# 64 more bytes in a small tensor, so that the tensors behind it lie 64 bytes further on

## The chip, the cores and the metric

One core of a Trainium2 chip runs the whole program. The metric is the device time of one execution in microseconds (us); lower is better. Three executions of the kernel before gave 1581.59, 1583.28 and 1583.49 us, a median of 1583.28 us.

## The reference

A chain of two transformer blocks on 256 tokens of width 1024, in float32.

```python
h = h + gla_mixer(rms_norm(h, a_norm), ...)            # gated linear attention, 4 heads
h = h + sqrelu_mlp(rms_norm(h, mlp_norm[0]), w1, w2)   # square(relu(x @ w1)) @ w2, hidden 4096
k_sh, v_sh = shared_kv(h, kv_norm, w_kv, k_norm)
h = h + diff_mixer(rms_norm(h, b_norm), k_sh, v_sh, ...)   # difference of two softmaxes, 8 heads
h = h + sqrelu_mlp(rms_norm(h, mlp_norm[1]), w1, w2)
# second block: three branches that are gated, summed and projected
merged = g0 * conv_branch(...) + g1 * ssd_branch(...) + g2 * windowed_attention(...)
h = h + merged @ w_mix_out
h = h + memory_cross_attention(rms_norm(h), rms_norm(mem), ...)
h = h + sqrelu_mlp(rms_norm(h, norm_mlp), w_mlp_up, w_mlp_down)
```

Nearly all of the arithmetic is in the products with weight matrices: 420 pieces ("chunks") of 1024 x 128 weights.

## The kernel before

**Layout.** Activations are held transposed: 128 partitions, and per partition 8 slices (`KC`) of 256 tokens (`T`). A weight chunk is 8 squares of 128 x 128.

**A product in three parts.** Both operands are split into a high part and a remainder. For each of the 8 slices PE does high weights times high activations (L396) and high weights times low activations (L397), both float32 with 256 columns. Then it does 8 bf16 products of the low weights (L406). A chunk is 16 float32 and 8 bf16 products, each with its own weight load. L440, L441 and L446 are the same three in the second half of an MLP; L423, L424 and L426 are the same three with the roles swapped (activations loaded as weights, weights moving), which is used where the result is wanted with tokens on the partitions.

**The stream of chunks.** SP loads weights into `raw`, a ring of four slabs of two chunks (L356, L368). ACT rounds a chunk to `w_hi` (L942), DVE subtracts to get `w_lo` (L1484), PE multiplies, DVE takes the sum out of PSUM. ACT may run 3 chunks ahead, and a slot of `w_hi` comes free when PE is done with the chunk four back. The order of the work on each engine is written out by hand; each engine's function (from L346 on for SP, then PE, ACT, DVE, POOL) walks through the same stages, with semaphores between them.

**Operand sets.** The activations for the products stand in two sets, XA and XB. Each has `both` (8 slices, each with 256 high and 256 low float32 numbers, so 2048 bytes a slice) and `bf` (8 slices of 512 bytes). ACT writes the high part and `bf` (L948, L949, L951, L952), DVE the low part (L1497, L1499).

**The arena.** All that lives for one stage only is cut out of one tensor, `arena`, of 81920 bytes a partition: masks, queries, keys, values, hidden activations (squared by POOL, L2120), the padded input of the 31-tap convolution, and so on. The convolution reads `c_in[:, i, k:k + T]` for each tap k: rows of 286 numbers (1144 bytes), starting 4 bytes further on with each tap. Six channel slices are done as products on ACT (L1190) and sums on POOL (L2150), two on DVE (L1764). The bias rows of the windowed attention are stored from the arena to DRAM once (L1098, issued from ACT's queue), and POOL fetches them back 16 times with a skew (L2162). The masks (L362) and the memory input are loaded into the arena once.

**Where the tensors lie.** Tensors are placed in the order in which they are declared (L117 to L166), one after the other. By the built program's list, in bytes within a partition:

| tensor | starts at | modulo 1024 | modulo 128 |
|---|---|---|---|
| raw | 16512 | 128 | 0 |
| w_hi | 49280 | 128 | 0 |
| w_lo | 65664 | 128 | 0 |
| H (the residual stream) | 73856 | 128 | 0 |
| con (constants) | 89184 | 96 | 96 |
| hn_sqb | 100096 | 768 | 0 |
| gains (64 bytes) | 104192 | 768 | 0 |
| arena | 104256 | 832 | 64 |
| xa_both | 186176 | 832 | 64 |
| xa_bf | 202560 | 832 | 64 |
| xb_both | 206656 | 832 | 64 |
| xb_bf | 223040 | 832 | 64 |
| small_hi, small_lo | 227136, 228160 | 832 | 64 |

`gains` holds four columns of scaled gains; only `gains[:, 0:4]` is ever written or read.

Of the kernel before, what the change touches and what calls it, by code (L numbers as in the profile page):

```python
# [22 lines left out]
P = 128  # L23
# [89 lines left out]
def program(nc, w_d, par_d, con_d, gm_d, x_d, mem_d, band_d, out_d):  # L113
    ctx = ExitStack()
    with ctx:
        def sb(name, shape, dt=F32):
            return ctx.enter_context(nc.sbuf_tensor(name, shape, dt))  # L117
# [22 lines left out]
        rtok_mem = sb("rtok_mem", [P, NT])  # L140
        hn_sqb = sb("hn_sqb", [P, 2, T])
        hn_rb = sb("hn_rb", [P, 2, T])
        gains = sb("gains", [P, 16])
        ARENA = 20480
        arena = sb("arena", [P, ARENA])
        ps = ctx.enter_context(nc.psum_tensor("ps", [P, 8, 512], F32))
# [2170 lines left out]
```

## Time and profile before

| | |
|---|---|
| median of 3 executions | 1583.28 us |
| the profiled execution | 1579.73 us |
| its span, first to last instruction | 1577.9 us |
| PE busy | 1426.4 us (90%) |
| PE weight loads busy | 1294.0 us (82%) |
| DVE busy | 1035.2 us (66%) |
| ACT busy | 889.3 us (56%) |
| POOL busy | 329.9 us (21%) |
| granted TensorE clock, mean | 0.959 |

The page gives the share of busy time, a row of 40 slices, the chain of work that ended last, and groups of instructions. A duration of an instruction is not its cost where instructions overlap: PE's matmuls are pipelined, and there the distance from one start to the next is what counts. It is read from the timeline.

### The profile page before, as it was taken

How to read it: one execution, taken by the hardware profiler on the slowest of the kernel's cores; microseconds unless marked ns; L12 is line 12 of the kernel's file. 1: busy time of each engine (PE TensorE's matmuls, PEld its weight loads, DVE VectorE, ACT ScalarE, POOL GpSimd, SP SyncE). 2: the span in 40 equal slices, each digit the busy share in tenths (PEclk: the TensorE clock that was granted, in tenths of full speed). 3: DMA queues.
4: the chain of work that ended last, by engine and by line, in shares of the span. 5: the costliest groups of instructions: out<-in, count | busy, mean ns of one | idle time of the engine just before them, and what ended most of it. 6: DMA issues, size and time to landing. Idle time of an engine off the chain costs nothing. (4 is left out here: it accounts for less than half of the span.)

```text
span 1577.9 us, 30012 instructions
## 1 busy us (share of the span) xinstructions
PE 1426.4 (90%) x11488; PEld 1294.0 (82%) x11488; DVE 1035.2 (66%) x1661; ACT 889.3 (56%) x1693; POOL 329.9 (21%) x334
## 2 busy tenths in 40 slices
PE   7987999989879999989877779898898979799999
PEld 6876999988757999989877667777777779599998
DVE  6794755566656666647999755568576666375555
ACT  4434655456556555548988655454565466365553
POOL 2000411132004111126878100004000004051111
PEclk9998999999987999979999989999999989999999
DMA  7320555545713555534434322234434335055552
GB/s 305 132 107 29 189 200 197 186 161 132 216 54 107 194 203 191 187 107 171 151 136 157 128 86 102 86 107 161 137 126 149 124 134 188 27 188 194 204 189 81
DMA packets 35603, 233.72 MB, mean 148 GB/s; under 512 B 4000, under 2 KB 7072, under 8 KB 8352
## 3 DMA queue, kind: packets, MB, share of 16 engines
q1 hardware_dynamic: 31104, 223.75, 39.8%
q10 hardware_dynamic: 3216, 4.19, 1.7%
q0 software_dynamic: 1168, 4.20, 0.9%
q8 instruction: 78, 1.28, 0.3%
q14 instruction: 37, 0.30, 0.1%
HBM read 227.93 MB, written 4.19 MB: 147 GB/s over the span
## 5 line engine op out<-in xcount | busy, mean ns | idle before, releaser
L1484 DVE TENSOR_TENSOR w_lo<-raw,w_hi 128x1024 bf16<-128x1024 f32 x420 | 536.1, 1277 | 242.4 <-ACT w_hi L942 239.0
L942 ACT CAST w_hi<-raw 128x1024 fp32r<-128x1024 f32 x420 | 438.7, 1047 | 351.7 <-PE ps L406 179.3
L396 PE MATMUL ps<-xa_both,w_hi 128*128 128x256 f32 x1808 | 464.9, 297 | 32.6 <-ACT w_hi L942 11.1
L397 PE MATMUL ps<-xa_both,w_hi 128*128 128x256 f32 x1808 | 439.7, 283 | 0.0
L396 PEld LDWEIGHTS ps<-xa_both,w_hi 128*128 128x128 f32 x1808 | 350.9, 194 | 44.1 <-issue 25.0
L397 PEld LDWEIGHTS ps<-xa_both,w_hi 128*128 128x128 f32 x1808 | 351.8, 195 | 0.6
L406 PE MATMUL ps<-xa_bf,w_lo 128*128 128x256 bf16 x1808 | 240.2, 277 | 21.4 <-DVE w_lo L1484 21.4
L406 PEld LDWEIGHTS ps<-xa_bf,w_lo 128*128 128x128 bf16 x1808 | 160.7, 99 | 49.3 <-DVE w_lo L1484 24.8
L440 PE MATMUL ps<-xb_both,w_hi 128*128 128x256 f32 x768 | 188.4, 288 | 0.0
L441 PE MATMUL ps<-xb_both,w_hi 128*128 128x256 f32 x768 | 180.0, 277 | 0.0
L396 PE MATMUL ps<-xb_both,w_hi 128*128 128x256 f32 x576 | 149.7, 299 | 13.5 <-DVE xb_both L1497 7.8
L2120 POOL TENSOR_TENSOR arena<-arena 128x256 f32<-128x256 f32 x96 | 68.2, 710 | 388.6 <-DVE arena L1553 388.6
L440 PEld LDWEIGHTS ps<-xb_both,w_hi 128*128 128x128 f32 x768 | 144.5, 188 | 1.1
L441 PEld LDWEIGHTS ps<-xb_both,w_hi 128*128 128x128 f32 x768 | 144.6, 188 | 0.0
L397 PE MATMUL ps<-xb_both,w_hi 128*128 128x256 f32 x576 | 141.3, 285 | 0.0
L2150 POOL TENSOR_TENSOR arena<-arena 128x512 f32<-128x512 f32 x90 | 127.4, 1417 | 51.1 <-ACT arena L1190 40.3
L396 PEld LDWEIGHTS ps<-xb_both,w_hi 128*128 128x128 f32 x576 | 112.8, 196 | 20.4 <-issue 12.4
L397 PEld LDWEIGHTS ps<-xb_both,w_hi 128*128 128x128 f32 x576 | 112.9, 196 | 0.2
L446 PE MATMUL ps<-xb_bf,w_lo 128*128 128x256 bf16 x768 | 100.5, 274 | 0.0
L2080 POOL TENSOR_TENSOR sumsq<-H 128x256 f32<-128x256 f32 x6 | 3.7, 612 | 400.7 <-DVE H L1521 370.0
L1190 ACT ACTIVATE arena<-arena,par 128x256 f32<-128x256 f32 x180 | 77.6, 497 | 6.6 <-POOL arena L2150 6.6
L406 PE MATMUL ps<-xb_bf,w_lo 128*128 128x256 bf16 x576 | 78.7, 282 | 0.0
(288 smaller groups left out, 1932.9 us busy)
## 6 DMA issues: line engine op xcount, KB each, us to landing
raw<-weights SPq DMA_DIRECT2D x210, 1024.0 KB, 4.8
band<-arena ACTq DMA_DIRECT2D x1, 3072.0 KB, 35.4
arena<-band POOLq DMA_DIRECT2D x8, 256.0 KB, 3.2
arena<-gla_masks SPq DMA_DIRECT2D x1, 1088.0 KB, 15.6
H<-x_t SPq DMA_DIRECT2D x2, 512.0 KB, 4.8
arena<-mem_t POOLq DMA_DIRECT2D x1, 1024.0 KB, 5.2
arena<-band POOLq DMA_DIRECT2D x8, 128.0 KB, 2.6
out_t<-H ACTq DMA_DIRECT2D x8, 128.0 KB, 2.0
```

The costliest lines, as they stand in the source:

```text
L396: mm(ps[:, bank, 0:T], w_hi[:, s, k], X.hi[:, k], start=k == 0, stop=False)
L397: mm(ps[:, bank, 0:T], w_hi[:, s, k], X.lo[:, k], start=False, stop=False)
L406: last = mm(ps[:, bank, 0:T], w_lo[:, s, k], X.bf[:, k], start=False, stop=k == KC - 1)
L440: mm(down_sums(n), w_hi[:, s, i], XB.hi[:, k], start=opens, stop=False)
L441: mm(down_sums(n), w_hi[:, s, i], XB.lo[:, k], start=False, stop=False)
L446: done = mm(down_sums(n), w_lo[:, s, i], XB.bf[:, k], start=False, stop=last and (k, n) == DOWN[j][-1] and j >= 4)
L942: nc.scalar.copy(w_hi[:, j % HI_SLOTS].rearrange("p k n -> p (k n)"), raw[:, j // 2 % RING, j % 2]).then_inc(hi_done, 1)
L1190: A(c_prod[:, a % PRODUCTS, i % 2], c_in[:, i, k:k + T], ACT.Copy, scale=w).then_inc(ca["prod"], 1)
L1484: TT(w_lo[:, j % HI_SLOTS].rearrange("p k n -> p (k n)"), raw[:, j // 2 % RING, j % 2], w_hi[:, j % HI_SLOTS].rearrange("p k n -> p (k n)" ...
L2080: G.tensor_tensor(sumsq[:], src[:, k], src[:, k], ALU.mult).then_inc(sq_step, 1)
L2120: G.tensor_tensor(m_sq[:, j % 2], m_relu[:, j % 2], m_relu[:, j % 2], ALU.mult).then_inc(sq_done, 1)
L2150: G.tensor_tensor(both, both, c_prod[:, a % PRODUCTS], ALU.add).then_inc(ca["add"], 1)
```

## The change

One number: `gains` becomes 32 columns wide instead of 16.

```diff
         hn_sqb = sb("hn_sqb", [P, 2, T])
         hn_rb = sb("hn_rb", [P, 2, T])
-        gains = sb("gains", [P, 16])
+        gains = sb("gains", [P, 32])
         ARENA = 20480
         arena = sb("arena", [P, ARENA])
```

`gains` stays at 104192 and takes 128 bytes. Everything declared after it (arena, XA, XB, small_hi, small_lo) starts 64 bytes later: at 896 instead of 832 modulo 1024, which is 0 instead of 64 modulo 128. `ps`, the accumulator, is another memory and does not move. No instruction is added, removed, reordered or reshaped on any engine: the five engines' lists of instructions are the same row for row.

## Rows read from the trace of the kernel before

**Rows 1.** The page, head and sections 1 and 2.
```profile
span 1577.9 us, 30012 instructions
...
PE 1426.4 (90%) x11488; PEld 1294.0 (82%) x11488; DVE 1035.2 (66%) x1661; ACT 889.3 (56%) x1693; POOL 329.9 (21%) x334
...
PEclk9998999999987999979999989999999989999999
```
**Rows 2.** The page, section 4: the chain that ended last.
```profile
PE 26%; DVE 3%; ACT 2%; issue 1%; DVEq 0%; ACTq 0%
```
**Rows 3.** Windows: busy us (and instructions) of each engine, clock, DMA share, GB/s.
```profile
150.00:350.00 200.00, 195.49 (x1712) 186.81 (x1711) 124.16 (x159) 108.15 (x162) 44.32 (x55) 0.99 0.54 190
350.00:400.00 50.00, 48.24 (x356) 42.75 (x355) 33.47 (x56) 33.69 (x67) 15.40 (x16) 0.94 0.52 115
400.00:480.00 80.00, 65.56 (x441) 49.98 (x439) 48.66 (x122) 45.39 (x140) 0.00 (x0) 0.87 0.41 127
```
**Rows 4.** Timeline, PE in an MLP: start us, us, engine, line, what.
```profile
300.71 1.05 PE L446 MATMUL ps<-xb_bf,w_lo 128*128 128x256 bf16 x8
...
302.07 0.28 PE L396 MATMUL ps<-xa_both,w_hi 128*128 128x256 f32 x1
302.18 0.28 PE L397 MATMUL ps<-xa_both,w_hi 128*128 128x256 f32 x1
...
303.32 0.28 PE L397 MATMUL ps<-xa_both,w_hi 128*128 128x256 f32 x1
...
303.44 1.05 PE L406 MATMUL ps<-xa_bf,w_lo 128*128 128x256 bf16 x8
```
**Rows 5.** One line each: min/median/max ns, first and last start, shapes. Weight loads.
```profile
L396 PEld LDWEIGHTS ps<-xa_both,w_hi x1808: 186/188/337, 10.8 to 1551.1; 128*128 128x128 f32 x181
...
L423 PEld LDWEIGHTS ps<-w_hi,xa_both x144: 186/188/199, 42.9 to 1114.0; 128*128 128x128 f32 x144
```
**Rows 6.** Timeline, PE with the roles swapped: weights move, activations are loaded.
```profile
405.00 0.28 PE L423 MATMUL ps<-w_hi,xa_both 128*128 128x256 f32 x1
...
406.47 0.28 PE L424 MATMUL ps<-w_hi,xa_both 128*128 128x256 f32 x1
```
**Rows 7.** Timeline, PE in the keys of the shared attention.
```profile
361.64 0.28 PE L396 MATMUL ps<-xa_both,w_hi 128*128 128x256 f32 x1
...
363.17 0.28 PE L397 MATMUL ps<-xa_both,w_hi 128*128 128x256 f32 x1
```
**Rows 8.** One line each: the convolution's taps, on ACT and on DVE.
```profile
L1190 ACT ACTIVATE arena<-arena,par x180: 492/495/512, 721.8 to 869.3; 128x256 f32<-128x256 f32 x180
...
L1764 DVE SCALAR_TENSOR_TENSOR ps<-arena,par,ps x58: 470/483/484, 758.4 to 859.8; 128x256 f32<-128x256 f32 x58
```
**Rows 9.** One line each: DVE sums into H, and products into the arena.
```profile
L1521 DVE TENSOR_TENSOR H<-ps,H x32: 415/424/425, 151.0 to 1399.4; 128x256 f32<-128x256 f32 x32
...
L1503 DVE TENSOR_TENSOR arena<-ps,rstd x102: 409/418/426, 32.8 to 1345.6; 128x256 f32<-128x256 f32 x102
```
**Rows 10.** One line each: POOL's squares, from H, and from the arena.
```profile
L2084 POOL TENSOR_TENSOR sqtmp<-H x42: 612/784/789, 154.6 to 1399.9; 128x256 f32<-128x256 f32 x42
...
L2120 POOL TENSOR_TENSOR arena<-arena x96: 612/722/779, 175.4 to 1553.1; 128x256 f32<-128x256 f32 x96
```
**Rows 11.** DMA issues: size of one, median us from issue to landing.
```profile
band<-arena ACTq DMA_DIRECT2D x1, 3072.0 KB, 35.4
...
arena<-gla_masks SPq DMA_DIRECT2D x1, 1088.0 KB, 15.6
```
**Rows 12.** One line each: issue of the bias rows, and the next user of them.
```profile
L1098 ACTq DMA_DIRECT2D band<-arena x1: 357/357/357, 383.8 to 383.8; - x1
...
L2140 POOL MEMSET arena<- x1: 303/303/303, 694.4 to 694.4; 128x240 f32 x1
```
**Rows 13.** Timeline, POOL fetches bias rows: start us, us, and idle before.
```profile
1132.96 0.72 POOL L2162 DMA_DIRECT2D arena<-band  x1 [27.94 <-DVE arena L1990]
1136.66 0.72 POOL L2162 DMA_DIRECT2D arena<-band  x1 [2.98 <-DVE arena L1990]
1147.05 0.72 POOL L2162 DMA_DIRECT2D arena<-band  x1 [9.66 <-DVE arena L1990]
```
**Rows 14.** Timeline, PE after the first MLP: the pauses, and the products behind them.
```profile
349.73 0.55 PE L396 MATMUL ps<-xa_both,w_hi 128*128 128x256 f32 x1 [4.45 <-DVE H L1537]
...
351.82 0.58 PE L396 MATMUL ps<-xa_both,w_hi 128*128 128x256 f32 x1
352.20 0.42 PE L397 MATMUL ps<-xa_both,w_hi 128*128 128x256 f32 x1
```

## Prediction

> **What bounds the kernel now.** I start at the page's head and its busy times: PE works 1426.4 of 1577.9 us, DVE 66%, ACT 56%, POOL 21% [rows 1]. The chain that ended last says the same for the part of the span that it is followed through, some 32%: 26 of these are PE's, 3 DVE's and 2 ACT's [rows 2]. The windows show two kinds of stage. In the first MLP PE is busy 195.49 of 200 us; in the differential attention only 65.56 of 80 us, with a granted clock of 0.87 [rows 3]. The reader should take from this that a change in the matmuls' pace counts in full in the MLPs and in part elsewhere, and that a change in DVE, ACT or POOL counts only in the attention stages and the convolution.
>
> Then the timeline inside an MLP. The group of 8 bf16 products starts at 300.71 and the next one at 303.44, so a chunk takes 2.73 us. From the product at 302.07 to the one at 303.32 are 11 steps: 1.25 / 11 = 113.6 ns from one float32 product to the next [rows 4]. That pace, 16 times per chunk and 420 chunks (6720 float32 products), is what the change could touch at the greatest price: 1 ns on each is 6.7 us if all lay on the path, 3.1 us for the 192 chunks of the three MLPs alone (192 x 16 = 3072 products).
>
> **The change part by part.** It adds and removes no instruction, DMA or wait. What it moves is the start of every operand that lies behind `gains`, from 64 to 0 modulo 128 bytes (from 832 to 896 modulo 1024). So the question is whether any engine's time depends on the start of an operand. The kernel itself contains operands of both kinds, and that is how each term can be read off the trace.
>
> *Moving operand of PE.* Before, XA and XB move (832 modulo 1024) against weights at 128. With the roles swapped, the weights at 128 move, and XA at 832 is loaded. From 405.00 to 406.47 are 13 steps of 1.47 / 13 = 113.1 ns [rows 6], against 113.6 [rows 4]. So a moving operand at 0 modulo 128 runs at the pace of one at 64. I take 0 ns. The bounds: the pace isn't 113.6 everywhere. In the keys' stage 13 steps take 1.53 us, 117.7 ns each [rows 7], with the same two tensors at the same addresses. That can't be a matter of address; what it is the rows don't tell, but it is the nearest price for a slower pace: 4.1 ns. The nearest for a faster one is the bf16 group, whose 8 products take 1.05 us, the last one's 0.27 or 0.28 included: (1.05 - 0.27) / 7 = 111 ns [rows 4], 2.6 ns less. Ends: -2.6 x 3072 = -8 us in the MLPs and -17 us in all; +4.1 x 3072 = +13 us and +28 us.
>
> *Weight loads.* With w_hi as weights the load takes 186/188 ns (least and median), with XA as weights 186/188 ns [rows 5]. Two kinds of start, one duration: 0.
>
> *ACT and DVE.* The taps of the convolution are the best natural experiment here. The 180 products on ACT start at 30 offsets, 4 bytes apart, in six rows that are themselves 1144 bytes apart: every multiple of 4 modulo 128 occurs. They take 492 to 512 ns, with a median of 495; the 58 on DVE take 470 to 484 [rows 8]. The whole spread over all starts is 20 and 14 ns, and a move of 64 bytes only permutes the starts among themselves. DVE's products into the arena (64 modulo 128) take 418 ns, its sums into H (0 modulo 128) 424 [rows 9]. I take 0. As an upper bound I let each of some 400 DVE instructions of this size become 6 ns slower or faster: 2.4 us, nearly all of it beside PE's work.
>
> *POOL.* Squares read from H and from the arena have the same least duration, 612 ns [rows 10]; the medians 784 and 722 are of different stages with different neighbours. I take 0; besides, POOL is idle 79% of the span [rows 1].
>
> *DMAs.* The weights' ring `raw` stands ahead of `gains` and doesn't move, nor do H's input and output. What moves are the masks, the memory input, 16 fetches of bias rows and one store of bias rows. The store takes 35.4 us, the masks 15.6 [rows 11]. The store is issued at 383.8; POOL's next step that waits for it is at 694.4 [rows 12], so it has 275 us to spare, and nothing would be late if it took twice as long. The bias fetches are issued 3.7 and 10.4 us apart, each after a step of DVE two units back [rows 13], and each waits for DVE rather than the other way round. I take 0 on the path. A rule speaks for a small loss here: the Trainium skill, page "DMA: Bandwidth & Descriptors", section "How a descriptor splits into AXI transactions", says that a read that doesn't start at a multiple of 256 bytes begins at the multiple below and pays for the bytes between, in beats of 32. The stored rows are 1536 bytes and start at 160 modulo 256, after the change at 224: 53 beats become 55, and my estimate from that page for the whole store is 35.4 x 2/53 = 1.3 us more. By it the sum would be +1.3 us if the store were on the path, and 0 where it stands.
>
> The sum: 0. For the profiled execution that means 1577.9 + 1.8 = 1579.7 us again. The median of the three runs lies 3.55 us above it; the forecast goes by the median: **1583.3 us**.
>
> **The rivals.** *The matmul's pace gets worse (slower).* After the change moving operands, loaded weights, `raw` and H all start at 0 modulo 128, where before the two that PE reads at the same time differed by 64. If PE reads both sides at once and two reads of one phase disturb each other, the place is the pair L396/L397 and L440/L441, and the price is up to the pace of the keys' stage: +13 us if only the MLPs feel it, +28 us if all do, 1596 to 1611 us, and 1603 as its middle. It decides from 0.5 ns a product on (0.5 x 6720 = 3.4 us). Against it: the weight slices are 512 bytes long, so successive ones start at 128 and 640 modulo 1024, and the pace within a chunk is steady. For it: no row here has both sides at 0 modulo 128 in this kind of product.
>
> *The matmul's pace gets better (faster).* The same place with the other sign: an operand at 64 modulo 128 needs one more access for its last piece, and the float32 pace of 113.6 comes down towards the 111 of bf16. That gives -8 to -17 us, 1566 to 1575 us. Against it: the swapped products move an operand that has the better start already and are no faster [rows 4, 6].
>
> *The clock falls otherwise (either sign).* After the first MLP PE pauses for 4.45 us, and two products behind the pause are 0.38 us apart, more than three times their usual distance [rows 14]; the mean granted clock of the stage is 0.94, against 0.99 in the MLP, and 0.87 in the attention behind it [rows 3]. Some stages hang on such pauses. A few nanoseconds elsewhere may shift where the clock falls: one chunk at three times the distance costs 16 x 0.26 = 4 us. That is an outcome of single executions; it would move the median only if it moved each run the same way: 1579 to 1588 us.
>
> *The change doesn't do what it says.* If other padding took up the 64 bytes, the addresses would be the old ones and the time 1583.3 us, the same as the forecast. The list of the built program's tensors speaks against it, and it costs the forecast nothing.
>
> **How the numbers follow.** About 0.2% (3.2 us) is what a measurement of this kernel can tell from no change; the three runs span 1.9 us. No effect: 0.76. Worse pace 0.09, better pace 0.09. The clock beyond 3.2 us: 0.03 on either side. So faster 0.12, same 0.76, slower 0.12. The forecast is 1583.3 us. The range 1578 to 1589 holds the case of no effect, most of the clock's, and a pace that is off by less than 1 ns; the rest of the two pace cases, some 0.15, stays outside.
>
> **What would show it.** Right: 113.6 ns between float32 products and 2.73 us per chunk in the MLPs, loads at 188 ns, L1190 at 495, L1521 at 424 and L1503 at 418, POOL's least at 612, all as before; PE busy within 3 us of 1426. Wrong: a chunk in an MLP of 2.67 or 2.80 us; or, if the time changes without that, an ACT, DVE or POOL group that reads the arena with a median off by over 5 ns, and its stage longer by as much. If only the stages around the pauses differ, it is the clock.

## The result: 1603.65 us, and the profile after

The kernel with the wider `gains` takes 1603.65 us (median of 4 executions, 1600.13 to 1605.35) against 1583.38 us (4 executions, 1581.59 to 1587.40) of the kernel before: a ratio of 1.0127 [1.0100, 1.0154]. It is 20 us slower, and outside the range of 1578 to 1589.

The page of the execution that was profiled (1605.35 us), head, busy times, clock, chain and two DMA issues:

```profile
span 1603.5 us, 30012 instructions
...
PE 1456.7 (91%) x11488; PEld 1320.0 (82%) x11488; DVE 1034.9 (65%) x1661; ACT 890.0 (55%) x1693; POOL 329.4 (21%) x334
...
PEclk9996999998987999989999989999999989899999
...
PE 25%; DVE 4%; ACT 2%; issue 1%; DVEq 0%; ACTq 0%
...
band<-arena ACTq DMA_DIRECT2D x1, 3072.0 KB, 35.5
...
arena<-gla_masks SPq DMA_DIRECT2D x1, 1088.0 KB, 15.0
```

Against [rows 1], the instructions are the same in number, and DVE, ACT and POOL work as long as before, to within 0.7 us. Only PE works longer: 30.3 us more in its products and 26 us more in its weight loads. The two DMAs take what they took [rows 11]. The mean granted clock of this execution is 0.952 against 0.959, so some of the difference between the two profiled executions is the clock's. But the execution of the changed kernel whose clock was 0.959 too took 1600.13 us, which is 20.4 more than the 1579.73 of the profiled one before.

The timeline of PE in an MLP of the changed kernel (start us, duration us, engine, line, what), to be held against [rows 4]:

```profile
300.86 0.28 PE L440 MATMUL ps<-xb_both,w_hi 128*128 128x256 f32 x1
...
301.93 0.28 PE L441 MATMUL ps<-xb_both,w_hi 128*128 128x256 f32 x1
```

These are 9 steps in 1.07 us, 118.9 ns from one float32 product to the next, where [rows 4] had 113.6. Taken as the mean over the last nine steps of the 16 float32 products of every chunk in the second halves of the MLPs (the "steady pace" from here on), it is 119.4 ns after and 113.3 ns before, and all 96 of these chunks are within 1 ns of it.

The same is seen more cheaply in a group's median duration. One line each, min/median/max ns, of the kernel before:

```profile
L441 PE MATMUL ps<-xb_both,w_hi x768: 276/276/283, 192.9 to 1573.1; 128*128 128x256 f32 x192
...
L424 PE MATMUL ps<-w_hi,xa_both x144: 276/279/284, 43.1 to 1114.2; 128*128 128x256 f32 x144
```

and of the changed kernel:

```profile
L441 PE MATMUL ps<-xb_both,w_hi x768: 278/282/284, 199.7 to 1598.7; 128*128 128x256 f32 x192
...
L424 PE MATMUL ps<-w_hi,xa_both x144: 278/283/284, 43.2 to 1132.1; 128*128 128x256 f32 x144
...
L441 PEld LDWEIGHTS ps<-xb_both,w_hi x768: 187/192/193, 199.6 to 1598.6; 128*128 128x128 f32 x192
L446 PE MATMUL ps<-xb_bf,w_lo x768: 272/273/284, 201.5 to 1599.6; 128*128 128x256 bf16 x192
```

A duration of 276 ns goes with a pace of 113.3, 279 with about 118, 282 or 283 with about 120; it moves by the same few nanoseconds as the pace, though it is more than twice as long. The float32 products are slower in every kind of chunk, and the weight load at L441 takes 192 ns (median) against 188. The bf16 products stay at 273 ns. And the row of L424 before holds a warning that I did not see: its median was 279 and not 276, so the swapped products were slower than the others in the kernel before already.

There is a second warning in that trace. Of the chunks that run at the full clock, not all of one kind have one pace: among 275 whole chunks at L396/L397, 238 run at 113.3 ns and 37 at 117.8, and the keys' stage [rows 7] is among the 37; among 25 swapped ones, 22 run at 117.8 and 3 at 113.3. The two operands lie in the same places modulo 256 bytes in both groups each time. So the addresses alone don't settle the pace of every single chunk. In the second halves of the MLPs, where the chunks follow each other without a pause, all 96 are at 113.3, which is why the steady pace is taken there.

The groups of the other engines whose operands moved:

```profile
L1190 ACT ACTIVATE arena<-arena,par x180: 492/495/513, 738.2 to 885.9; 128x256 f32<-128x256 f32 x180
...
L1503 DVE TENSOR_TENSOR arena<-ps,rstd x102: 410/420/426, 32.8 to 1363.5; 128x256 f32<-128x256 f32 x102
...
L1521 DVE TENSOR_TENSOR H<-ps,H x32: 419/425/425, 156.3 to 1420.5; 128x256 f32<-128x256 f32 x32
...
L2120 POOL TENSOR_TENSOR arena<-arena x96: 612/725/782, 181.7 to 1578.2; 128x256 f32<-128x256 f32 x96
```

None of their medians is off by more than 3 ns from [rows 8, 9, 10].

**The sum.** In a chunk of an MLP's second half the 15 steps between float32 products went from 1800 to 1868 ns, and the step from the last of them to the first bf16 product from 117 to 122: 73 ns a chunk. Times 420 chunks that would be 30.6 us, which is close to the 30.3 by which PE's busy time rose. That the two agree is partly chance, because a swapped chunk loses only 20 to 30 ns, most of them, and the float32 products of a chunk at the lower clock none. Taken product by product from the two traces, the float32 products of the chunks account for 25.9 us: 7.0 in the second halves of the MLPs (96 x 73 ns), 19.5 in the other whole chunks and -0.6 in the swapped ones, one of which ran at the lower clock before and none after. The bf16 products give -1.3 us, and the remaining 5.7 us are PE's other products, of which 210 instead of 184 fell at the lower clock. The span rose by 25.6 us and not by 30.3; the rest was hidden in stages where PE waits for others anyway. The medians are 20.3 us apart, less than the spans, since the profiled execution was the slowest of the four after the change, and the one before it (1579.73 us) faster than the four that its median is taken from. Where the loss was hidden can be read from landmarks in the changed kernel:

```profile
L1098 ACTq DMA_DIRECT2D band<-arena x1: 362/362/362, 397.0 to 397.0; - x1
...
L2140 POOL MEMSET arena<- x1: 304/304/304, 712.8 to 712.8; 128x240 f32 x1
...
L2162 POOL DMA_DIRECT2D arena<-band x16: 720/722/764, 1121.2 to 1266.3; - x16
...
L1537 DVE TENSOR_TENSOR H<-ps,H x12: 678/684/692, 350.1 to 1600.0; 128x512 f32<-128x512 f32 x12
```

and the two of these in the kernel before that [rows 12] do not have:

```profile
L2162 POOL DMA_DIRECT2D arena<-band x16: 720/722/764, 1103.5 to 1250.1; - x16
...
L1537 DVE TENSOR_TENSOR H<-ps,H x12: 676/683/692, 339.4 to 1574.4; 128x512 f32<-128x512 f32 x12
```

| landmark | before, us | after, us | later by |
|---|---|---|---|
| first sum of an MLP into H (L1537), behind the first MLP | 339.4 | 350.1 | 10.7 |
| store of the bias rows (L1098) | 383.8 | 397.0 | 13.2 |
| padding of the convolution (L2140) | 694.4 | 712.8 | 18.4 |
| first fetch of bias rows (L2162) | 1103.5 | 1121.2 | 17.7 |
| last DVE sum of a projection (L1521) | 1399.4 | 1420.5 | 21.1 |
| last sum of an MLP (L1537) | 1574.4 | 1600.0 | 25.6 |

The first 340 us, nearly all PE, lose 10.7 us; the stages between 694 and 1103, which hold the convolution, lose nothing; the last MLP loses 4.5.

### The profile page after: what moved, and what is told of

The parts are those of the page before. It is cut to its first block and busy times, and to the rows that moved or that the text cites. A ratio compares the mean times of both kernels' runs of the same rounds, so it can differ in the third digit from the quotient of the medians.

```text
span 1603.5 us, 30012 instructions
## 1 busy us (share of the span) xinstructions
PE 1456.7 (91%) x11488; PEld 1320.0 (82%) x11488; DVE 1034.9 (65%) x1661; ACT 890.0 (55%) x1693; POOL 329.4 (21%) x334
## 5 line engine op out<-in xcount | busy, mean ns | idle before, releaser
L396 PE MATMUL ps<-xa_both,w_hi 128*128 128x256 f32 x1808 | 479.1, 301 | 31.5 <-ACT w_hi L942 10.1
L397 PE MATMUL ps<-xa_both,w_hi 128*128 128x256 f32 x1808 | 454.2, 288 | 0.0
L396 PEld LDWEIGHTS ps<-xa_both,w_hi 128*128 128x128 f32 x1808 | 354.3, 196 | 42.5 <-issue 23.9
L397 PEld LDWEIGHTS ps<-xa_both,w_hi 128*128 128x128 f32 x1808 | 356.8, 197 | 0.6
L440 PE MATMUL ps<-xb_both,w_hi 128*128 128x256 f32 x768 | 195.0, 292 | 0.0
L441 PE MATMUL ps<-xb_both,w_hi 128*128 128x256 f32 x768 | 186.8, 282 | 0.0
L396 PE MATMUL ps<-xb_both,w_hi 128*128 128x256 f32 x576 | 154.1, 303 | 12.6 <-DVE xb_both L1497 7.3
L440 PEld LDWEIGHTS ps<-xb_both,w_hi 128*128 128x128 f32 x768 | 145.7, 190 | 1.1
L441 PEld LDWEIGHTS ps<-xb_both,w_hi 128*128 128x128 f32 x768 | 146.6, 191 | 0.0
L397 PE MATMUL ps<-xb_both,w_hi 128*128 128x256 f32 x576 | 146.2, 290 | 0.0
L396 PEld LDWEIGHTS ps<-xb_both,w_hi 128*128 128x128 f32 x576 | 114.1, 198 | 19.1 <-issue 12.0
L397 PEld LDWEIGHTS ps<-xb_both,w_hi 128*128 128x128 f32 x576 | 114.7, 199 | 0.2
L1190 ACT ACTIVATE arena<-arena,par 128x256 f32<-128x256 f32 x180 | 77.6, 497 | 6.6 <-POOL arena L2150 6.6
## 6 DMA issues: line engine op xcount, KB each, us to landing
band<-arena ACTq DMA_DIRECT2D x1, 3072.0 KB, 35.5
```

The lines of the kernel that those rows point to most:

```text
L396: mm(ps[:, bank, 0:T], w_hi[:, s, k], X.hi[:, k], start=k == 0, stop=False)
L397: mm(ps[:, bank, 0:T], w_hi[:, s, k], X.lo[:, k], start=False, stop=False)
L440: mm(down_sums(n), w_hi[:, s, i], XB.hi[:, k], start=opens, stop=False)
L441: mm(down_sums(n), w_hi[:, s, i], XB.lo[:, k], start=False, stop=False)
L1190: A(c_prod[:, a % PRODUCTS, i % 2], c_in[:, i, k:k + T], ACT.Copy, scale=w).then_inc(ca["prod"], 1)
```

## Experiments

The suspect after the traces is PE's pace in float32 products. What about an address decides it? In this kernel PE reads two things at once: the weights that it loads for the next product and the operand that moves for the present one. (In the changed kernel, for example, the load for a product of L441 starts at 300.86 us and takes 0.19 us, beside the product of L440 that starts then.) I call **distance** the start of the operand set minus the start of `w_hi`, in bytes. It was 186176 - 49280 = 136896 before, which is 192 modulo 256 (704 modulo 1024); after the change it is 0 modulo 256 (768 modulo 1024). A slice of an operand set (2048 bytes, halves of 1024), a weight square (512) and a slot of weights (4096) are all whole multiples of 256, so the distance modulo 256 is one number for a whole kernel. Where the roles are swapped (L423, L424) it has the other sign.

**Is it the sets alone, and is it an absolute place?** The first kernel leaves the arena at 832 and moves only the sets. The second moves everything from `raw` on by 64 bytes, so that all places change and no distance does.

e1_sets_only:
```diff
+        pad = sb("pad", [P, 16])
         XA, XB = XSet("xa"), XSet("xb")
```
e2_all_moved:
```diff
+        pad = sb("pad", [P, 16])
         raw = sb("raw", [P, RING, 2, D])
```

> The arena stays at 832 modulo 1024; only the operand sets behind it (XA, XB, small_hi, small_lo) move 64 bytes, to 896. Theory A (PE's float32 products slow down by where the moved activations lie against the loaded weights): all of the loss is here, 120 ns between float32 products and 1604 us. Theory B (PE depends on the start of the activations alone, 0 instead of 64 modulo 128): the same, 120 ns and 1604 us. Theory C (it is the arena: ACT, DVE, POOL or the bias and mask DMAs): 113.6 ns and 1583 us.

> Everything from raw on moves 64 bytes: activations at 896 modulo 1024 as in the change, weights w_hi at 192, so that their distance is 704 modulo 1024 as before the change. Theory A (distance): as the kernel before, 113.6 ns and 1583 us. Theory B (start of the activations alone): as the change, 120 ns and 1604 us. If ACT's, DVE's or SP's use of raw and w_hi at 64 modulo 128 costs anything, it shows here too, as L942 or L1484 off by over 5 ns.

e1: 1602.48 us, ratio 1.0099 [1.0081, 1.0118], steady pace 119.4. e2: 1586.91 us, ratio 1.0010 [0.9987, 1.0033], pace 113.3. (Each ratio is to executions of the kernel before that were made beside it on the same chip; their medians lie between 1583.4 and 1587.0 us.) One line each, first of e1, then of e2 (L442 is L441 there):

```profile
L442 PE MATMUL ps<-xb_both,w_hi x768: 278/282/283, 196.4 to 1595.1; 128*128 128x256 f32 x192
```
```profile
L442 PE MATMUL ps<-xb_both,w_hi x768: 276/276/283, 192.8 to 1569.6; 128*128 128x256 f32 x192
```

The sets alone bring the loss, and the arena is not needed for it. With everything at the new places, the sets at 896 included, there is no loss. So it is not where the moving operand lies, but how far it lies from the loaded one; e3 below moves the loaded one instead.

**By which period?** Two kernels that change the distance in other ways: e3 declares `gains` ahead of `w_hi`, which moves the weights and leaves the sets where they were (distance 128 modulo 256, and 0 modulo 128 as after the change); e4 makes `gains` 48 columns wide (distance 64 modulo 256, and 64 modulo 128 as before it).

e3_weights_moved:
```diff
+        gains = sb("gains", [P, 16])
         w_hi = sb("w_hi", [P, HI_SLOTS, KC, P], F32R)
...
-        gains = sb("gains", [P, 16])
```
e4_sets_128:
```diff
-        gains = sb("gains", [P, 16])
+        gains = sb("gains", [P, 48])
```

> Arena and operand sets stay at 832 as before; w_hi, w_lo, H and the small tensors move 64 bytes (w_hi at 192 modulo 1024), so the distance from weights to activations is 640 instead of 704. Theory A (distance): another pace than 113.6 ns is possible; if 704 is a good place and 768 a bad one by a period of 128, 640 is bad too: 120 ns, 1604 us. Theory B (start of the activations alone): 113.6 ns and 1583 us.

> gains is 48 columns wide: arena and operand sets at 960 modulo 1024, which is 64 modulo 128 again, 128 bytes further than before. If the period is 128 (by A or by B alike): 113.6 ns and 1583 us. If it is longer (256 or 1024): no need for either value, and the pace can be anywhere from 109 to 122 ns, 1560 to 1612 us.

e3: 1602.01 us, 1.0087 [1.0070, 1.0104], pace 119.2. e4: 1598.42 us, 1.0067 [1.0051, 1.0084], pace 117.8. The rows of e4:

```profile
L441 PE MATMUL ps<-xb_both,w_hi x768: 278/279/280, 198.8 to 1592.2; 128*128 128x256 f32 x192
...
L424 PE MATMUL ps<-w_hi,xa_both x144: 276/276/415, 44.0 to 1130.1; 128*128 128x256 f32 x144
```

e3 shows that moving the weights costs as much as moving the sets. e4 rules out a rule modulo 128: it has the old distance by that rule, and is slow. Its second row is the best evidence in the study. The swapped products, at 279 ns before, are at 276 in e4 (20 of 25 chunks at the full clock at 113.3 ns, where 3 of 25 were before), while the others have become slow (266 of 275 whole chunks at 117.8 ns). With distance 64 for the others, the swapped ones stand at -64, which is 192 modulo 256: the place of the fast products of the kernel before. And in the kernel before the swapped ones stood at -192, which is 64, and ran, all but three chunks, at the 117.8 ns of e4's others.

Four more widths of `gains` ask whether the pattern repeats after 256 bytes or only after 1024: 64 in s896 (the edit shown), 80 in s960, 96 in s0, 144 in s192.

```diff
-        gains = sb("gains", [P, 16])
+        gains = sb("gains", [P, 64])
```

> gains 64 columns wide: the distance from w_hi to the activations is 896 modulo 1024 (384 modulo 512), a value not measured yet. If the distance sets the pace (theory A) with a period of 512, the four distances so far (640, 704, 768, 832) cover 128 to 320 modulo 512 and this one is new: anything from 109 ns (the bf16 pace, 1565 us) to 120 ns. If the period were 256, it would be as 640: 119.0 ns, 1602 us.

> gains 80 wide: distance 960 modulo 1024 (448 modulo 512). If the period of theory A were 256, it would be as 704, the kernel before: 113.4 ns, 1583 us. If it is 512: new, 109 to 120 ns.

> gains 96 wide: distance 0 modulo 1024, so that a weight square and the activations start at the same place modulo 512. If the period of theory A were 256, it would be as 768, the change: 119.6 ns, 1604 us. If reads conflict when they are near each other, this should be among the slowest, 120 ns or more; if two reads of one place are good, the fastest, 109 to 112 ns.

> gains 144 wide: distance 192 modulo 1024, 512 bytes further than before. The weight squares alternate between 128 and 640 modulo 1024, so theory A says that a move of 512 changes nothing: steps in the MLPs of 113.4 ns on the mean as before, 1583 us. If the period is 1024 it can be anything.

| kernel | distance modulo 1024 | modulo 256 | steady pace, ns | median, us | ratio |
|---|---|---|---|---|---|
| before | 704 | 192 | 113.3 | | |
| after | 768 | 0 | 119.4 | 1603.65 | 1.0127 [1.0100, 1.0154] |
| e4 | 832 | 64 | 117.8 | 1598.42 | 1.0067 [1.0051, 1.0084] |
| s896 | 896 | 128 | 119.2 | 1602.25 | 1.0126 [1.0069, 1.0184] |
| s960 | 960 | 192 | 113.3 | 1586.97 | 1.0019 [0.9997, 1.0042] |
| s0 | 0 | 0 | 119.4 | 1603.56 | 1.0135 [1.0082, 1.0187] |
| e3 | 640 | 128 | 119.2 | 1602.01 | 1.0087 [1.0070, 1.0104] |
| s192 | 192 | 192 | 113.3 | 1583.59 | 1.0005 [0.9982, 1.0029] |

The period is 256: three kernels at 192 agree, two at 0, two at 128. In none of the five kernels at 0 or 128 (e1 is the fifth) does a single float32 chunk at the full clock run at 113.3 ns. At 192 and 64, 113.3 and 117.8 occur side by side; what changes from one to the other is which of them is the rule. e3 and s896 even have the same least, median and greatest duration, though one moved the weights and the other the sets. The row of s896:

```profile
L441 PE MATMUL ps<-xb_both,w_hi x768: 274/282/287, 199.4 to 1597.2; 128*128 128x256 f32 x192
```

**Four distances in one run.** If the distance decides, and not some state of a whole run, then slots of `w_hi` that lie at different distances must show their own paces in one execution, chunk by chunk. Here a slot is made 64 bytes longer, so that slots 0 to 3 stand at 192, 128, 64 and 0.

```diff
-        w_hi = sb("w_hi", [P, HI_SLOTS, KC, P], F32R)
+        w_hi = sb("w_hi", [P, HI_SLOTS, KC * P + 16], F32R)[:, :, 0:KC * P].rearrange("p s (k n) -> p s k n", k=KC)
```

> Each of the four slots of w_hi is 64 bytes longer, so that the slots stand at distances of 192, 128, 64 and 0 modulo 256 from the activations in one and the same program. Theory A with its period of 256, as PE's own two reads: a chunk's pace goes by its slot, c modulo 4: 113.4, 119, 117.7, 119.6 ns, and the time lies between, about 1583 + (117.4 - 113.4) / (119.6 - 113.4) x 20 = 1596 us. Theory D (other engines' accesses to w_hi or raw slow PE down, by their place against the activations): ACT writes a slot three further on, DVE reads one or two behind that, for 2.3 of the 2.7 us, so the pace would change within a chunk or by another slot than the one PE loads from.

It took 1599.59 us, 1.0092 [1.0062, 1.0121], and the steady paces by slot are 113.3, 120.1, 117.8 and 120.0 ns. The timeline of it, PE: last products of a chunk in slot 3, its bf16 group, then the same of the next chunk, in slot 0.

```profile
206.01 0.28 PE L441 MATMUL ps<-xb_both,w_hi 128*128 128x256 f32 x1
...
206.97 0.28 PE L441 MATMUL ps<-xb_both,w_hi 128*128 128x256 f32 x1
207.09 1.05 PE L446 MATMUL ps<-xb_bf,w_lo 128*128 128x256 bf16 x8
...
208.80 0.28 PE L441 MATMUL ps<-xb_both,w_hi 128*128 128x256 f32 x1
...
209.70 0.28 PE L441 MATMUL ps<-xb_both,w_hi 128*128 128x256 f32 x1
```

Eight steps take 0.96 us in slot 3 (120 ns) and 0.90 us in slot 0 (113 ns), under 3 us apart, on the same engine with the same neighbours. This also answers the clock: a lower clock would not pick every fourth chunk.

**Is there a better place than 192?** The kernel before would then be beaten. Five kernels look at finer steps or take the high and low halves apart. Four of them are e5 with another number: a slot is 8 numbers longer in e6 (`gains` 48) and e7 (`gains` 16), and 4 longer in e9 (`gains` 56) and e11 (`gains` 72). In e10 a slot is 16 longer, and the halves of a set become two tensors with a pad between them, 64 bytes apart in either set modulo 256:

```diff
-                self.both = sb(name + "_both", [P, KC, 2, T], F32R)
-                self.hi, self.lo = self.both[:, :, 0], self.both[:, :, 1]
+                self.hi = sb(name + "_hi", [P, KC, T], F32R)
+                sb(name + "_pad", [P, apart])
+                self.lo = sb(name + "_lo", [P, KC, T], F32R)
...
+        XA = XSet("xa", 16)
+        XB = XSet("xb", 48)
```

> Slots 32 bytes longer, sets moved so that slots 0 to 3 stand at 192, 160, 128 and 96 modulo 256. Theory A: slot 0 at 113.4 ns, slot 2 at 119.0; slots 1 and 3 are new. If the memory is divided at 64 bytes, slot 1 is like one of its neighbours (113.4 or 119.0) or between; under 113 ns in slot 1 would be a better place than any so far.

> Slots 32 bytes longer, sets so that slots 0 to 3 stand at 64, 32, 0 and 224 modulo 256. Theory A: slot 0 at 117.7 ns, slot 2 at 119.6; slots 1 and 3 are new, and slot 3 (224) is the other neighbour of the good place at 192.

> Slots 16 bytes longer, sets so that slots 0 to 3 stand at 224, 208, 192 and 176 modulo 256. Theory A: slot 0 at 118.2 ns, slot 2 at 113.3; slots 1 and 3 lie between their neighbours if the effect is one of distance in 16-byte pieces. A slot under 113 ns would be the better place that a faster kernel needs; I expect none, since 160 and 224 are both worse than 192.

> High and low activations in tensors of their own, with w_hi's slots 64 bytes longer, so that (hi, lo) stand modulo 256 at (192,0), (128,192), (64,128), (0,64) for XA in slots 0 to 3, and at (0,192), (192,128), (128,64), (64,0) for XB. Theory A with each product bound by its own distance: the pace is near the mean of the two paces measured alone, e.g. (113.3 + 120) / 2 = 116.7 ns for (192,0). If what counts is how far the load has to wait behind the product before it, alternating places could give the loads room: a slot under 113 ns, down to 109, and then a faster kernel than before is possible.

> Slots 16 bytes longer, gains 72 wide, so that slots 0 to 3 really stand at 224, 208, 192 and 176 modulo 256 from the activations. Theory A: slot 0 at 118.2 ns, slot 2 at 113.3. If the good place is one of 64 bytes' alignment only, slots 1 and 3 are at 117 to 120; if it is a broad one, one of them is at 113.3. None under 113.3 means that no move by 16 bytes gives a faster kernel than before.

| kernel | distances of slots 0 to 3 | steady paces, ns | one run, us |
|---|---|---|---|
| e6 | 192, 160, 128, 96 | 113.3, 117.0, 118.6, 120.5 | 1602.61 |
| e7 | 64, 32, 0, 224 | 117.8, 117.8, 119.4, 118.2 | 1601.16 |
| e9 | 160, 144, 128, 112 | 118.3, 120.6, 119.1, 120.0 | 1606.48 |
| e11 | 224, 208, 192, 176 | 118.2, 117.8, 113.3, 118.8 | 1593.2 |
| e10 | high and low at different distances | 117.2, 117.6, 117.5, 119.6 | 1606.81 |

e9 is partly a miss: the expectation on record names the distances 224 to 176, but I had added up wrongly, and the slots stood at 160 to 112. e11 is the kernel that e9 was meant to be. It shows that the good place is sharp: 16 bytes to either side of 192 the pace is 118 or 119. e10 set high and low 64 bytes apart, so that every chunk has two distances: 192 for one half does not help when the other stands elsewhere (117.2 for the pair 192 and 0, near the 116.7 that the mean of the two would be). Away from 192 one distance can differ by about a nanosecond from kernel to kernel: 160 ran at 117.0 in e6 and at 118.3 in e9, and 0 at 120.0 in e5 and at 119.4 in e7.

**PE alone, at 64 distances.** The last open points are whether another engine has a part in it, and whether any distance gives less than 113.3. The kernel before is followed by 64 more chunks of 16 float32 and 8 bf16 products, whose weights start 4 bytes further each time (those of the bf16 products too); no other engine works meanwhile, and nobody reads the bank they go to.

```diff
+            pe.wait_ge(bank_free, CHUNKS)
+            hi_flat = w_hi[:].rearrange("p s k n -> p (s k n)")
+            for i in range(64):
+                for k in range(KC):
+                    at = slice(i + k * P, i + (k + 1) * P)
+                    mm(ps[:, 0, 0:T], hi_flat[:, at], XA.hi[:, k], start=k == 0, stop=False)
+                    mm(ps[:, 0, 0:T], hi_flat[:, at], XA.lo[:, k], start=False, stop=False)
...
```

> The kernel before, with 64 further chunks of products behind the last one, when ACT, DVE and POOL have ended: 16 float32 products each with weights read from w_hi at a start that is 4 bytes further on each time, so that the distance modulo 256 goes from 192 down by 4 a chunk, and 8 bf16 products with w_lo likewise; their sums go to a bank that nobody reads. About 64 x 2.8 = 180 us more. Theory A (PE's own weight load against its moving operand): the paces of the runs with all engines come back with PE alone: 113.3 ns at 192, about 118 at 176, 160, 208 and 224, 119 to 120 at 128 and 0, 118 at 64. Theory D (collision with other engines): PE alone has one pace at every distance, 109 to 113 ns. For bf16 I expect 109 ns everywhere. A distance with a pace under 113 ns would allow a faster kernel.

It took 1763.71 us. The window of the added part (busy us and instructions of PE, PEld, DVE, ACT, POOL; clock; DMA share; GB/s):

```profile
1590.00:1760.00 170.00, 170.00 (x1467) 162.49 (x1466) 0.00 (x0) 0.00 (x0) 0.00 (x0) 1.00 0.00 1
```

PE is alone, at a granted clock of 1.00, with hardly any DMA (1 GB/s). Its timeline, the bf16 groups that end chunks 0 to 4:

```profile
1585.17 1.05 PE L924 MATMUL ps<-xa_bf,w_lo 128*128 128x256 bf16 x8
...
1587.96 1.05 PE L924 MATMUL ps<-xa_bf,w_lo 128*128 128x256 bf16 x8
...
1590.74 1.05 PE L924 MATMUL ps<-xa_bf,w_lo 128*128 128x256 bf16 x8
...
1593.48 1.05 PE L924 MATMUL ps<-xa_bf,w_lo 128*128 128x256 bf16 x8
...
1596.26 1.05 PE L924 MATMUL ps<-xa_bf,w_lo 128*128 128x256 bf16 x8
```

The chunks take 2.79, 2.78, 2.74 and 2.78 us: the third of these, at distance 180, is as fast as one at 192. The float32 paces of some of the 64 distances over the last nine steps, in ns, from one chunk each:

| distance | 192 | 188 | 184 | 180 | 176 | 172 | 168 | 164 | 144 | 128 |
|---|---|---|---|---|---|---|---|---|---|---|
| pace | 113.3 | 118.2 | 118.6 | 113.3 | 118.8 | 120.1 | 113.3 | 118.6 | 121.1 | 118.3 |

| distance | 96 | 76 | 64 | 52 | 32 | 16 | 0 | 248 | 224 | 196 |
|---|---|---|---|---|---|---|---|---|---|---|
| pace | 119.8 | 114.9 | 117.8 | 123.0 | 116.7 | 117.1 | 120.0 | 115.6 | 118.1 | 120.7 |

Over these nine steps three distances of the 64 reach 113.3 (192, 180 and 168), none less; 52 is the worst with 123.0. The bf16 products run at 109.2 ns at all 64 (from the second step of a group on). So no other engine is needed for the effect, and none of the distances tried is faster than that of the kernel before.

A chunk can also find its pace on the way. The chunk at 76, whose 114.9 in the table is a mixture:

```profile
1664.20 0.28 PE L921 MATMUL ps<-xa_both,w_hi 128*128 128x256 f32 x1
...
1665.14 0.28 PE L921 MATMUL ps<-xa_both,w_hi 128*128 128x256 f32 x1
...
1665.82 0.28 PE L921 MATMUL ps<-xa_both,w_hi 128*128 128x256 f32 x1
```

The first eight of these steps take 0.94 us (118 ns each), the last six 0.68 us (113 ns). At 180 and 168 it is alike: the 113.3 comes after the first six steps only (1816 and 1814 ns for the 15 steps of the chunk), while at 192 in the MLPs it is there after four (1800 ns). So 76 belongs with the good distances by its end, and since 113.3 occurs now and then at 64 too (9 of 275 whole chunks in e4), one chunk doesn't prove that 180, 168 or 76 would be good for a whole kernel. No run puts a kernel there.

**The change kept, the loss taken away.** `gains` stays at 32 columns and the arena at 896, and a pad ahead of the sets restores 192.

```diff
-        gains = sb("gains", [P, 16])
+        gains = sb("gains", [P, 32])
...
+        pad = sb("pad", [P, 48])
         XA, XB = XSet("xa"), XSet("xb")
```

> gains 32 wide as in the change, so the arena stands at 896 modulo 1024; 192 bytes of padding behind the arena put XA and XB 256 bytes further than before, a distance of 192 modulo 256 as before. Theory A: 113.4 ns between float32 products and a time equal to the kernel before within 0.3%: the loss of the change is gone with its edit still in. If the arena's place matters by itself: part of the 1% stays, with 113.4 ns.

1584.43 us (10 executions, 1581.59 to 1591.10) against 1586.25 of the kernel before on the same chip: ratio 0.9997 [0.9973, 1.0021]. The steady pace is 113.4, PE's busy time 1428.1 us (1426.4 before, 1456.7 after).

```profile
L442 PE MATMUL ps<-xb_both,w_hi x768: 275/276/283, 195.0 to 1575.2; 128*128 128x256 f32 x192
```

The whole loss is gone with the change still in. What the arena's move costs is nothing that these 10 executions can show.

## Why the prediction was wrong

The mechanism that came true is the rival "The matmul's pace gets worse", to which I gave 0.09: both sides that PE reads at once, at L396/L397 and L440/L441, in a bad relation to each other. Its middle was 1603 us and the median is 1603.65, though this is partly luck: its worst price was 4.1 ns a product, and the true one is 6.1 in the MLPs (113.3 to 119.4), of which some was hidden in the stages between them. Its condition, both starts at 0 modulo 128, is not the true one either: e4 keeps the old difference of 64 modulo 128 and is slow.

**The step that failed** is "*Moving operand of PE*": "So a moving operand at 0 modulo 128 runs at the pace of one at 64. I take 0 ns." It fails in three ways.

- It took the start of one operand for what matters. The rows compared, [rows 4] and [rows 6], swap the operands, so both starts change at once, and what they share is the pair. The runs show that the pair matters: by the distance, with its sign, modulo 256. The comparison could not answer the question that I put to it.
- Even as it stood, it was read off one chunk. [rows 6] gives 113.1 ns, but it is one of the 3 exceptions among the 25 swapped chunks at the full clock in the kernel before; the other 22 run at 117.8 ns, and the median of L424 is 279 ns against 276 of L441 in the row above. One look at that median would have shown that swapping the roles costs 3 to 4 ns, in a kernel where the only thing that is swapped is which address is loaded and which moves.
- Of the keys' stage at 117.7 ns [rows 7] I said that it "can't be a matter of address". It is true that the addresses are those of [rows 4]. But 37 of 275 whole chunks in the kernel before run at this pace, and it is the very pace that becomes the rule at a distance of 64: what the stage shows is the second of two paces that this placement allows. Why a chunk takes one or the other stays open. The keys' chunk begins with a step of 0.30 us, behind a product of another kind, but of the 27 whole chunks at the full clock that begin with such a step, 14 run at 113.3. As the bound for a slower pace it was too low: the change gave 119.4, and the worst distance is 123.0.

"*Weight loads* ... 0" failed as well, in the median: 188 to 192 ns at L441. No run separates it from the products' pace; in e4, where the pace is 117.8, the loads are at 188 still.

**For and against, in the rival.** "For it: no row here has both sides at 0 modulo 128 in this kind of product" was the sentence to act on. Where the new state occurs nowhere in the trace, the trace cannot price it, and 0.76 for "no effect" was far too sure. "Against it: the weight slices are 512 bytes long, so successive ones start at 128 and 640 modulo 1024, and the pace within a chunk is steady" spoke against nothing: 512 is two whole periods of 256.

**What held.** ACT and DVE at 0: L1190 at 495 again, L1503 at 420 (418 before) and L1521 at 425 (424). POOL at 0: its least is 612 again. DMAs at 0 on the path: the store takes 35.5 us against 35.4. My estimate from the Trainium skill, page "DMA: Bandwidth & Descriptors", section "How a descriptor splits into AXI transactions", was 1.3 us more for it; the trace does not show it. The rival "better pace" fell, with the 113.3 ns of the kernel before the least of all 64 distances. "The clock falls otherwise" is no part of the pace: e5 has slow and fast chunks 3 us apart, and e12 has slow ones at a clock of 1.00. Its price was also misread: the 0.38 us between two products in [rows 14] is the step at a chunk's start, and a steady step at the lower clock is 213 ns, less than twice the usual and not three times. That the change does what it says is shown by e1. The test that I had named for the case of error, "a chunk in an MLP of 2.67 or 2.80 us", gave 2.80 (2.73 + 0.073).

**On the size of what can be told.** I had put it at 0.2%. Executions of the kernel before spread from 1576 to 1591 us over these comparisons, and intervals of 8 to 10 executions are still 0.23% wide on each side. The prediction was wrong by far more; but "no change" in e2, e8, s960 and s192 means within that.

## What to carry to other kernels

Where PE runs float32 products back to back, each with its own weight load, the start of the moving operand minus the start of the loaded one, modulo 256, is a property of the kernel like any other: note it, keep it when a tensor ahead of either grows, and put a pad back where it was lost (48 columns, or 192 bytes, here). Check it in the median duration of one matmul line (276 against 279 to 283 ns here), or from start to start in the timeline; a fault of 5% in the pace hides well in a profile whose instructions and waits are all the same. And when a question is about two operands that are read together, look for evidence with that pair; one that changes both sides at once, or one chunk, is none.

## What the runs showed of the hardware

- The pace of float32 products of 256 columns with a weight load each depends on the distance between the two operands, from 113.3 to 123.0 ns. In kernels whose distances differ by whole multiples of 256 bytes it is the same. It is sharp: 16 bytes off 192 it is 117.8 and 118.8 (24 chunks each in e11), 4 bytes off it is 118.2 (one chunk in e12). The worst case costs 9%.
- At one distance there can be two paces, 113.3 and 117.8 ns. At 192, 238 whole chunks of the kernel before have the one and 37 the other; at 64 (e4) it is 9 and 266. At 0 and 128 the lower one doesn't occur. What makes a chunk take one or the other is open.
- bf16 products of the same shape do not depend on the distance (109.2 ns at all 64).
- The Trainium skill, page "TensorE: Matmul & The Clock Gate", section "Step-by-step: what each phase is for", says that PE has two independent read ports, and that loading the next tile's weights does not take bandwidth from the running product. For bf16 the runs agree. For float32 they show that the two reads are not independent in every placement: with PE alone on the core, e12 has a pace that depends on where the loaded operand lies against the moving one.
- In these runs it is seen at the higher clock level only. After the pause behind the first MLP the changed kernel runs a chunk at the lower level (1.2 GHz), as its timeline shows:

```profile
370.02 0.42 PE L397 MATMUL ps<-xa_both,w_hi 128*128 128x256 f32 x1
...
372.79 0.42 PE L396 MATMUL ps<-xa_both,w_hi 128*128 128x256 f32 x1
```

- These are 13 steps in 2.77 us, 213.1 ns each, and 256 columns at 1.2 GHz take 213.3. Over all float32 steps of chunks at that level (140 to 163 in each trace) the mean pace is 213.4 to 213.6 ns before, after, in e3 and in e4, at distances of 192, 0, 128 and 64. At 2.4 GHz 256 columns would take 106.7 ns; bf16 comes to 109.2, and no float32 pace below 113.3. So what the distance costs may be time that the reads need at the higher level and for which the lower one has room. That is an inference from these paces, and no run tests it.
- Open: why the period is 256 bytes, why just 192 (and in single chunks 180, 168 and 76) is good, and what picks between the two paces at one distance. No run here tests what lies behind the numbers.
